# Attention heads of a layer scored two at a time, with the turns of their probabilities and their outputs moved to other slots

## What is computed

```python
# x (1, 256, 2048); HEAD_DIM_2 = 64; A_HEADS = 8, B_HEADS = 8, C_HEADS = 16
A: scores = q @ k.T * 64**-0.5 + t5 bias, |key - query| <= 128, one sink logit in the softmax
B: scores = q @ k.T * 64**-0.5 + relative bias, 16-column neighbourhood of a 64-wide grid
C: scores = rope(q) @ rope(k).T * gains, every key
o  = softmax(scores) @ v            # per head, 256 queries by 256 keys
y  = concat(group_norm(oA), group_norm(oB), group_norm(oC)) @ w_o
```

## Time and profile before

| | |
|---|---|
| time, median of 3 runs | 3412.58 us (3410.4 to 3422.04) |
| the profiled execution | 3420.76 us |
| its span, first to last instruction | 3419.1 us |
| TensorE busy | 3290.6 us, 96% of the span |
| VectorE busy | 2242.9 us, 66% |
| ScalarE busy | 1438.2 us, 42% |
| GpSimd busy | 157.6 us, 5% |
| granted TensorE clock, mean | 0.975 |
| memory traffic | 681.68 MB, mean 199 GB/s |

### The profile page before, as it was taken

The page is one execution under the profiler, slowest core; times in us unless marked ns, Lnnn a source line. Parts: engine busy times, 40 slices in busy tenths (PEclk is TensorE's granted clock), DMA queues, the critical chain, the costliest instruction groups (busy, mean ns, idle before and its releaser), DMA issues.

```text
span 3419.1 us, 63534 instructions
## 1 busy us (share of the span) xinstructions
PE 3290.6 (96%) x27286; PEld 3188.0 (93%) x27286; DVE 2242.9 (66%) x2339; ACT 1438.2 (42%) x1422; POOL 157.6 (5%) x292
## 2 busy tenths in 40 slices
PE   5999979999999999999999999999999999999998
PEld 5998879999999998878999999999887999999998
DVE  5797877666666586567655555557567765555555
ACT  3253334444444454545443344334444534433433
POOL 2111100000001000011000000000011000000000
PEclk7899999999999999999999999999999999999999
DMA  9788768666666554334555555555344465555553
GB/s 381 281 318 304 270 250 269 219 205 214 207 208 220 185 162 138 124 127 157 195 189 192 196 193 189 195 185 174 123 124 136 162 197 193 189 195 196 189 192 135
DMA packets 320749, 681.68 MB, mean 199 GB/s; under 512 B 14768, under 2 KB 21620, under 8 KB 320164
## 3 DMA queue, kind: packets, MB, share of 16 engines
q1 hardware_dynamic: 286272, 562.74, 49.9%
q0 software_dynamic: 31232, 109.07, 8.8%
q10 hardware_dynamic: 3108, 7.89, 0.6%
HBM read 677.47 MB, written 7.94 MB: 200 GB/s over the span
## 4 chain that ended last, share of the span: by engine, by line
PE 87%; DVE 6%; DMA 2%; ACT 2%; issue 2%; POOL 0%; ACTq 0%; DVEq 0%; POOLq 0%; SPq 0%
PE G L688 52%; PE Dn L688 34%; DVE w_lo L1231 2%; PE Dn L691 1%; DVE ada_acc L1356 1%; DMA zT<-in_w_ada 1%; ACT w_hi L2172 1%; DMA ada_raw<-in_w_ada 1%; DVE sq L1280 1%; DMA raw<-in_w_in 0%; DMA raw<-in_w_out 0%; DVE sq L1947 0%; DVE xT L1961 0%; DMA ada_x<-in_w_ada 0%; PE G L691 0%
## 5 line engine op out<-in xcount | busy, mean ns | idle before, releaser
L688 PE MATMUL G<-h_hi,w_hi 128*128 128x256 f32 x5760 | 1617.4, 281 | 10.0 <-DVE w_lo L1231 5.3
L1231 DVE TENSOR_TENSOR w_lo<-raw,w_hi 128x2048 fp32r<-128x2048 f32 (+2 forms) x536 | 1219.3, 2275 | 609.3 <-ACT w_hi L2172 608.0
L2172 ACT CAST w_hi<-raw 128x2048 fp32r<-128x2048 f32 (+2 forms) x536 | 1017.2, 1900 | 1421.4 <-DMA raw<-in_w_down 424.1
L688 PE MATMUL G<-h_lo,w_hi 128*128 128x256 f32 x5760 | 1603.4, 278 | 0.0
L688 PE MATMUL G<-h_hi,w_lo 128*128 128x256 f32 x5760 | 1603.0, 278 | 0.0
L688 PEld LDWEIGHTS G<-h_hi,w_hi 128*128 128x128 f32 x5760 | 1090.9, 189 | 33.7 <-issue 29.0
L688 PEld LDWEIGHTS G<-h_lo,w_hi 128*128 128x128 f32 x5760 | 1090.9, 189 | 0.4
L688 PEld LDWEIGHTS G<-h_hi,w_lo 128*128 128x128 f32 x5760 | 1090.2, 189 | 0.0
L688 PE MATMUL Dn<-act_hi,w_hi 128*128 128x256 f32 x2752 | 763.2, 277 | 7.3 <-DVE act_lo L1765 7.3
L688 PE MATMUL Dn<-act_lo,w_hi 128*128 128x256 f32 x2752 | 762.8, 277 | 0.0
L688 PE MATMUL Dn<-act_hi,w_lo 128*128 128x256 f32 x2752 | 762.7, 277 | 0.0
(11 more groups left out here) (259 smaller groups left out, 1677.8 us busy)
## 6 DMA issues: line engine op xcount, KB each, us to landing
raw<-in_w_up SPq DMA_DIRECT2D x128, 1024.0 KB, 5.4
raw<-in_w_down SPq DMA_DIRECT2D x128, 1024.0 KB, 5.0
raw<-in_w_in SPq DMA_DIRECT2D x88, 1024.0 KB, 5.3
ada_raw<-in_w_ada POOLq DMA_DIRECT2D x120, 512.0 KB, 6.5
raw<-in_w_ffn_gate SPq DMA_DIRECT2D x44, 1024.0 KB, 5.1
raw<-in_w_ffn_up SPq DMA_DIRECT2D x44, 1024.0 KB, 5.1
raw<-in_w_ffn_down SPq DMA_DIRECT2D x44, 1024.0 KB, 5.0
raw<-in_w_o SPq DMA_DIRECT2D x32, 1024.0 KB, 5.0
```

The costliest lines, as they stand in the source:

```text
L688: return nc.tensor.matmul(o, lhsT, rhs, start=start, stop=stop, skip_group_check=True)
L1231: v.tensor_tensor(w_lo[j][:, 0:m], raw[j][:, 0:PIECE_K * n], w_hi[j][:, 0:m], ALU.subtract).then_inc(lo_done, 1)
L2172: s.copy(w_hi[j][:, 0:PIECE_K * n], raw[j][:, 0:PIECE_K * n]).then_inc(hi_done, 1)
```

## The change

The heads of layers 0 and 1 are started two at a time, an even head h and the odd one after it. In most slots that start two, the scores are issued by turns: first query tile of the one head, first tile of the other, second tile of the one, second of the other (`score_pair`). The first head of a pair is turned one slot later and the second two slots later, in the slot that starts the next pair; the outputs of both are made in that later slot, behind its scores, and copied out by one instruction. Where the next pair starts in the very next slot, and at the last pair, both heads are turned and output one slot later ("quick" in the code); then turns and scores alternate by head as before. Each entry of `SLOTS2` now has three lists: heads turned, heads output, heads started. The slots of the first block's eight heads (`SLOTS1`) keep their contents. VectorE's and ScalarE's hooks follow the lists: probabilities and copies of probabilities by the heads turned, output copies by the heads output, row maxima and exponentials by the heads started.

By slots, after the change: started 12, 14, 16, 18, 20, 22, 24, 25, 27, 29, 31, 33, 34, 36, 38, 39, two each. Turns and nothing else of the heads: 13, 15, 17, 19, 21, 23, 26, 28, 30, 32, 35, 37.

```diff
 def head_slots():
-    starts = {12: "C12", 13: "C13", 14: "C14", 15: "C15", 16: "C8", 17: "C9", 18: "C10", 19: "C11",
-              20: "C4", 21: "C5", 22: "C6", 23: "C7", 24: "C0", 25: "C1", 26: "C2 C3",
-              27: "B4", 28: "B5", 29: "B6", 30: "B7", 31: "B0", 32: "B1", 33: "B2 B3",
-              34: "A0", 35: "A1", 36: "A2", 37: "A3", 38: "A4 A5", 39: "A6 A7"}
+    starts = {12: "C12 C13", 14: "C14 C15", 16: "C8 C9", 18: "C10 C11", 20: "C4 C5", 22: "C6 C7", 24: "C0 C1",
+              25: "C2 C3", 27: "B4 B5", 29: "B6 B7", 31: "B0 B1", 33: "B2 B3", 34: "A0 A1", 36: "A2 A3",
+              38: "A4 A5", 39: "A6 A7"}
+    slots, seq = {p: ([], [], []) for p in range(12, 41)}, 0
+    for p, names in starts.items():
...
+        slots[p][2].extend(pair)
+        quick = p + 1 in starts or p + 1 == 40
+        slots[p + 1][0].extend(pair if quick else pair[:1])
+        if not quick:
+            slots[p + 2][0].extend(pair[1:])
+        slots[p + 1 if quick else p + 2][1].extend(pair)
...
+            def score_pair(new, base):
+                for H, kind, h in new:
+                    score_waits(kind, h, base + H)
+                for t in range(QT):
+                    for H, kind, h in new:
+                        i = score(H, kind, h, t)
+                        if t == QT - 1:
+                            i.then_inc(qk_done, 1)
...
-            def slot(done, new, base):
+            def slot(trans, outs, new, base):
+                pair = len(new) == 2 and len(trans) < 2
-                for n in range(max(len(done), len(new))):
-                    if n < len(done):
-                        H, kind, h = done[n]
+                for n in range(max(len(trans), len(new))):
+                    if n < len(trans):
+                        H, kind, h = trans[n]
                         finish(H, kind, h, base + H, 0)
-                    if n < len(new):
+                    if n < len(new) and not pair:
                         H, kind, h = new[n]
                         scores(H, kind, h, base + H)
-                if done:
-                    misc_open(out_name(done), mbase[0])
-                    for H, kind, h in done:
+                if pair:
+                    score_pair(new, base)
+                if outs:
+                    misc_open(out_name(outs), mbase[0])
+                    for H, kind, h in outs:
                         i = finish(H, kind, h, base + H, 1)
                     i.then_inc(misc_w, 1)
...
-                    for p, (done, new) in SLOTS2.items():
+                    for p, (done, _, _) in SLOTS2.items():
                         hook(p + 1, slot, done, [], l * HEADS2 + HEADS1)
...
-                    for p, (done, new) in SLOTS2.items():
-                        hook(p + 1, copy_probs, done, hb)
-                        hook(p + 1, copy_out, done)
+                    for p, (trans, outs, _) in SLOTS2.items():
+                        hook(p + 1, copy_probs, trans, hb)
+                        hook(p + 1, copy_out, outs)
```

More of the change, by code:

```diff
@@ L133, in head_slots @@
 def head_slots():
-    starts = {12: "C12", 13: "C13", 14: "C14", 15: "C15", 16: "C8", 17: "C9", 18: "C10", 19: "C11",
[3 rows of a table removed]
[L139 to L143, removed]
-            seq += 1
[L145 to L148, removed]
+    starts = {12: "C12 C13", 14: "C14 C15", 16: "C8 C9", 18: "C10 C11", 20: "C4 C5", 22: "C6 C7", 24: "C0 C1",
[3 more added lines that the diff above has]
+    for p, names in starts.items():
+        pair = []
+        for name in names.split():
+            pair.append((seq, name[0], int(name[1:])))
+            seq += 1
+        slots[p][2].extend(pair)
[4 more added lines that the diff above has]
+        slots[p + 1 if quick else p + 2][1].extend(pair)
+    assert seq == 32
     return slots
@@ L866, in scores @@
                     pe.wait_ge(fm_ready, h + 1)
[L867 to L870, removed]
                     return
@@ L899, in slot @@
                         i = finish(H, kind, h, base + H, 1)
                     i.then_inc(misc_w, 1)
-            for p, (done, new) in SLOTS1.items():
-                hook(p, slot, done, new, 0)
+            for p, (trans, outs, new) in SLOTS1.items():
+                hook(p, slot, trans, outs, new, 0)
             for half in range(4, 10):
@@ L1111, in _ @@
                         hook(p, v_turn, z, evac)
-                    for p, (done, new) in SLOTS2.items():
-                        hook(p, slot, done, new, l * HEADS2 + HEADS1)
+                    for p, (trans, outs, new) in SLOTS2.items():
+                        hook(p, slot, trans, outs, new, l * HEADS2 + HEADS1)
                     for kind in "CBA":
@@ L1678, in _ @@
             last1 = MIX1_PIECES
-            for p, (done, new) in SLOTS1.items():
+            for p, (done, _, new) in SLOTS1.items():
                 hook(p, slot, done, [], 0)
@@ L2035, in _ @@
                         hook(QK_SS_AT[b_] + 1, qk_read, b_)
-                    for p, (done, new) in SLOTS2.items():
+                    for p, (_, _, new) in SLOTS2.items():
                         hook(p + 1, slot, [], new, l * HEADS2 + HEADS1)
@@ L2382, in split_hi1 @@
                 s.copy(h_hi[:, 4 * q:4 * q + 4, :], zT[:, z:z + 4, :]).then_inc(y1_hi, 1)
-            for p, (done, new) in SLOTS1.items():
+            for p, (_, _, new) in SLOTS1.items():
                 hook(p + 2, exps, new, 0)
-            for p, (done, new) in SLOTS1.items():
-                hook(p + 1, copy_probs, done, 0)
+            for p, (trans, _, _) in SLOTS1.items():
+                hook(p + 1, copy_probs, trans, 0)
             for q in (2, 3):
@@ L2405, in _ @@
             hook(25, v_copy1, [6, 7])
-            for p, (done, new) in SLOTS1.items():
-                hook(p + 1, copy_out, done)
+            for p, (_, outs, _) in SLOTS1.items():
+                hook(p + 1, copy_out, outs)
             hook(36, split_hi1, 0, 3)
@@ L2725, in _ @@
                 gp.wait_ge(mod_ready, 10)
-                order = [(k, h) for p in sorted(SLOTS2) for _, k, h in SLOTS2[p][1] if k != "C"]
+                order = [(k, h) for p in sorted(SLOTS2) for _, k, h in SLOTS2[p][2] if k != "C"]
                 for l in range(LAYERS):
```

25 lines of the change are left out of this document (16 added, 9 removed).

## The result

The changed kernel takes 3372.41 us (median of 6 runs, 3365.09 to 3382.15) against 3413.45 us for the kernel before on the same chip (6 runs, 3410.4 to 3422.04): ratio 0.988, 95% interval 0.9865 to 0.9894, a gain of 41 us or 1.2%. The forecast was a gain of 24 us, a time of 3389 and a range of 3375 to 3401. The profiled execution took 3368.84 us; its span is 3367.2.

The account below looks back on a forecast made before the run. TensorE bounds the kernel, busy throughout the C heads, partly waiting in the B and A heads. Per layer 13.9 - 0.3 + 11.6 - 6.7 - 6.8 = 11.7; 24 us off gives 3389 us, range 3375 to 3401.

Parts of the forecast that it names:

- C stretch: Slots 12 to 27, C heads: 13.9 us of TensorE's time saved per layer, 0.3 lost to VectorE.
- TensorE's work in the B and A stretch: Slot 27 to the end of piece 41: TensorE's work falls from 39.0 to 27.4, 11.6 us saved per layer.
- waits there: B and A heads: TensorE waits longer for VectorE ahead of turns, net 6.7 us per layer.
- low clock there: B and A heads: waits at slots 30 and 32 bring two more slow stretches per layer, 6.8 us for both.
- Overlap of scores: New pair slots: two heads on opposite row halves overlap fully, so a pair's scores take 1.07 us.
- overlap of outputs: New pair slots: outputs on opposite column halves overlap, so a pair's outputs take 1.02 us.
- the hidden copy: New pair slots: the 0.59 us copy of the second head's turned probabilities runs under the pair's 1.07 us of scores.
- the end at 2.4 us dearer: Twelve turn-only slots per layer: with the same row and column mode switches they would cost 2.4 us more.
- The rival without new slow stretches: B and A heads: slots 30 and 32 bring no low clock, 2 x 6.8 comes back: 3375 us; chance 0.15.
- The rival with a clock that stays low: Slots 28 to 38: clock stays low between waits, 51 us more per layer: 3491 us; chance 0.04.
- the rival with longer stretches: B and A heads: all four slow stretches last 9.9 us, costing 19.8 per layer: 3400 us; chance 0.11.

Follow-up runs that it names:

- blocks: Changed kernel with a pair's scores issued in blocks, both query tiles of one head and then of the other, instead of by turns: 3370.54 us, ratio 0.9867.
- outs_apart: Changed kernel with each head of a pair output in the slot in which it is turned: 3428.39 us, ratio 1.0045 to the kernel before.
- next_slot: Changed kernel with both heads of a pair turned and output one piece after their start: 3441.19 us, ratio 1.0071 to the kernel before.
- late_max: Changed kernel with the second head's row maximum and exponentials one piece later where the next slot starts nothing: 3363.95 us, ratio 0.9839.

## Why the forecast was too small, by its own steps

For sizes I set three profiles of each kernel (six layers) against the prediction, since the table shows that one is not enough. Per layer:

| term | forecast | measured |
|---|---|---|
| C stretch | -13.6 | -14.8 |
| TensorE's work in the B and A stretch | -11.6 | -11.1 |
| waits there | +6.7 | +5.7 |
| low clock there | +6.8 | -0.7 |
| sum | -11.7 | -20.9 |

The work is the stretch less its waits and half of its low clock, taking matmuls at half speed there. The low clock of the kernel before lies between 3 and 17 us in six layers, so that its term is known to about 1 us only (an estimate from this scatter). Two layers give 41.8 us. The timed medians differ by 41, but the three profiled executions of each kernel by 48: the other 6 us lie ahead of slot 12 (4) and behind the mixers (2), where both kernels do the same. That the sum meets the timed difference so closely is partly luck.

- **C stretch: right**, and 1.2 us better than forecast. Overlap of scores, overlap of outputs and the hidden copy are all as the prediction read them from slots 26, 39 and 27, and `blocks`, `outs_apart` and `next_slot` show each. Turns alone cost 0.35 and not 0.44, 1.0 us for twelve slots; the end at 2.4 us dearer is excluded. In two of three profiles of the kernel before, layer 1 also has a stretch of 3 us at low clock in the C part, which the forecast didn't count as a cost; it makes 0.5 of the 14.8.
- **B and A work: right** within 0.5.
- **Waits: right** in place and order: 4.42, 2.42, 2.28, 2.10, 0.76, 1.44, 0.22, 1.68 against 4.7, 3.1, 2.3, 2.09, 0.9, 1.6, 0.9, 1.6. Slots 30 and 37 were put 0.7 too high. The wait of 1.35 to 1.56 us at slot 31, in two of these six layers and in `blocks`, was not forecast. The two waits of 0.46 for copied outputs went, as said. That they cost more than they need is shown by `late_max`.
- **The clock: this step failed.** "Slots 30 and 32 would wait 3.1 and 2.3 us: two more per layer, each costing half its length." It took a slow stretch to belong to a wait of 2.1 us or more, one by one, and the two existing ones as fixed. The runs show one stretch behind slots 30 and 32 together, of 3.2 us; none left behind slot 34; and one of 5.0 to 6.7 behind slot 28. The sum per layer went from 10.4 us (3 to 17 in the six layers) to 8.9 us, and half of that difference is 0.7 gained where 6.8 was charged. That is 7.5 of the 9.2 us per layer by which the forecast missed; it was not luck with a single execution, since each of the eight layers of the changed kernel has two stretches and not four. The profile shown was the one with most low clock, 16.7 us in layer 0, and layer 1 already had a shorter stretch behind the very same wait.
- The rival without new slow stretches gave 3375 and came nearest, though it is right by half only: one did come, and an old one went. The rival with a clock that stays low has nothing for it; no stretch in the B and A part of any kernel outlasted 10.2 us. Its sum takes 13.4 us for four stretches where the rival with longer stretches takes 14.3; that changes its 3491 by 2 us.

Left open is what decides whether a wait is followed by the lower clock. Wait lengths between 1.9 and 2.4 us don't, and the executions that differ run the same instructions around a wait. In the changed kernel the second stretch follows slot 30 where the first lasted 5.0 to 5.4 us (five layers) and slot 32 where it lasted 6.5 or 6.7 (three), so the cases are linked; how, no run here shows. The stretch of the C part came with no wait at all, behind sixteen matmuls of two columns, and is missing behind the same matmuls in the second profile. Open too is a difference of some 4 us ahead of slot 12, where both kernels do the same: it starts at 1311.7 to 1314.4 us before and 1308.2 to 1309.6 after, but at 1304.6 to 1318.2 in the kernels with other edits, and I take it for scatter.

## What to carry to other kernels

Read the price of running two small matmul jobs on opposite halves of the array from any place where the kernel already does so, and put other work between the turns and the outputs that need their copy: with outputs straight behind their turns the whole gain was gone. Long waits can be taken from one profile, since they repeat to about 0.2 us, while short ones come and go with the clock. Take the clock from several profiles, and charge a new wait of 2 us with a share of a slow stretch and not with a whole one: here two more such waits added none. When heads are paired, split the other engines' share of the pair again: moving half of VectorE's work by one piece gave another 0.3 to 0.4%.

## What the runs showed of the hardware

- Matmuls with contraction 64 on opposite row halves overlap whether they are issued by turns or in blocks of four: eight in 1.06 and 1.07 us, where four take 1.06. Eight outputs on opposite column halves take 1.02, where four take 1.00.
- Granted clock: behind waits of 1.9 to 2.4 us it was 0.50 in some executions and 1.00 in others, for the same kernel and slot. The slow stretches of the B and A parts lasted 2.9 to 10.2 us in all kernels; behind the waits of 4.4 us, 5.0 to 6.7 us in all eight cases of the table. In two of three profiles of the kernel before, a stretch of 3.3 us fell in the C part of layer 1, where TensorE had not waited at all.
- Where an output follows its own turns, the copy by ScalarE (0.58 us) leaves TensorE idle for 0.72 to 0.78 us.
